# Layer 1's head periods: an SSM tile's turn counts and lag products move ahead in the vector queue, and the second tile's expansion drops its wait for the first

## What is computed

```
for l in range(DEPTH):                       # two layers
    h = rms_norm(x, norm_g[l]); z = h @ w_in[l]
    ... o_na, o_dl, o_m: 6 + 6 + 4 heads ...
    x = x + concat(o * silu(gate)) @ w_out[l]
# second block, s5_mixer:
ab = exp(lam * dt)                           # 64 groups x 64 states, complex
bu = B_bar u;  s_t = ab * s_(t-1) + bu_t;  y = C s + d_skip * u
```

## Time and profile before

| what | value |
|---|---|
| median of 3 runs | 2592.64 us (2587.49 to 2593.14) |
| the profiled execution's own time | 2586.36 us |
| its span | 2584.7 us |
| PE busy | 2476.3 us, 96% of the span |
| DVE, ACT, POOL busy | 65%, 47%, 24% |
| chain that ended last | PE 69%, DVE 15%, issue 7%, ACT 5% |
| head periods of layer 1 | about 552 to 1030 us |
| PE busy there (552 to 1024) | 441.55 of 472 us, granted clock 0.97 |

### The profile page before, as it was taken

One profiled execution on the slowest core, in us unless ns is written; L12 is line 12 of the kernel. 1 busy time (PEld: TensorE's weight loads), 2 busy tenths in 40 slices (PEclk: granted clock), 3 DMA queues, 4 the chain that ended last, 5 costly groups with the idle time before them and its releaser, 6 DMA issues.

```text
span 2584.7 us, 50520 instructions
## 1 busy us (share of the span) xinstructions
PE 2476.3 (96%) x18072; PEld 2348.0 (91%) x18072; DVE 1691.9 (65%) x2556; ACT 1220.9 (47%) x1819; POOL 628.6 (24%) x1047
## 2 busy tenths in 40 slices
PE   7999999989999999999988999999999999999999
PEld 7899999989899999998888999999888888888888
DVE  7876666567777777667777766565555555555555
ACT  5344544445555555555665434444544444444443
POOL 3300031358778886220010222011000000000000
PEclk9999999999999999999999999999999999999999
DMA  6655575555555555555454777565666676767764
GB/s 234 209 181 195 175 221 178 186 173 174 166 177 182 186 184 188 159 165 191 141 169 152 234 234 239 201 218 173 191 191 187 187 187 186 186 186 187 187 185 157
DMA packets 217449, 484.85 MB, mean 188 GB/s; under 512 B 22760, under 2 KB 120724, under 8 KB 217088
## 3 DMA queue, kind: packets, MB, share of 16 engines
q1 hardware_dynamic: 182912, 415.29, 52.6%
q0 software_dynamic: 13216, 37.93, 4.7%
q10 hardware_dynamic: 21216, 30.22, 3.6%
HBM read 455.00 MB, written 31.08 MB: 188 GB/s over the span
## 4 chain that ended last, share of the span: by engine, by line
PE 69%; DVE 15%; issue 7%; ACT 5%; POOL 2%; ACTq 1%; DVEq 0%; DMA 0%; POOLq 0%
PE z_ps L1987 12%; PE z_ps L1988 12%; PE z_ps L1989 12%; PE z_ps L2323 6%; PE z_ps L2324 6%; PE z_ps L2329 6%; DVE w_lo L1297 5%; ACT w_hi L717 2%; PE o_ps L2358 1%; PE o_ps L2357 1%; PE o_ps L2356 1%; PE v_ps L2357 1%; PE v_ps L2356 1%; PE p_ps L2357 1%; PE v_ps L2358 1%
## 5 line engine op out<-in xcount | busy, mean ns | idle before, releaser
L1297 DVE TENSOR_TENSOR w_lo<-w_raw,w_hi 128x1024 fp32r<-128x1024 f32 x520 | 634.8, 1249 | 335.4 <-ACT w_hi L717 333.1
L1987 PE MATMUL z_ps<-x_hi,w_hi 128*128 128x256 f32 x2816 | 822.1, 292 | 16.9 <-DVE w_lo L1290 14.4
L1988 PE MATMUL z_ps<-x_lo,w_hi 128*128 128x256 f32 x2816 | 805.3, 286 | 0.0
L1989 PE MATMUL z_ps<-x_hi,w_lo 128*128 128x256 f32 x2816 | 804.9, 286 | 0.0
L717 ACT ACTIVATE w_hi<-w_raw 128x1024 fp32r<-128x1024 f32 x520 | 533.1, 1051 | 262.5 <-PE z_ps L1989 216.5
L1987 PEld LDWEIGHTS z_ps<-x_hi,w_hi 128*128 128x128 f32 x2816 | 549.0, 195 | 26.9 <-issue 18.8
L1988 PEld LDWEIGHTS z_ps<-x_lo,w_hi 128*128 128x128 f32 x2816 | 549.3, 195 | 1.0
L1989 PEld LDWEIGHTS z_ps<-x_hi,w_lo 128*128 128x128 f32 x2816 | 548.9, 195 | 0.0
L1877 DVE TENSOR_TENSOR w_lo<-w_raw,w_hi 128x1024 fp32r<-128x1024 f32 x262 | 320.8, 1225 | 314.8 <-ACT w_hi L1141 314.7
L1141 ACT ACTIVATE w_hi<-w_raw 128x1024 fp32r<-128x1024 f32 x262 | 277.7, 1060 | 427.9 <-PE z_ps L2329 272.5
L2323 PE MATMUL z_ps<-w_hi,x_hi 128*128 128x512 f32 x704 | 275.1, 391 | 0.6 <-DVE res L1853 0.6
(11 more groups left out here) (382 smaller groups left out, 4131.5 us busy)
## 6 DMA issues: line engine op xcount, KB each, us to landing
w_raw<-in_w SPq DMA_DIRECT2D x704, 512.0 KB, 4.3
w_raw<-in_w SPq DMA_DIRECT2D x80, 384.0 KB, 4.8
res<-tab_d POOLq DMA_DIRECT2D x32, 384.0 KB, 4.5
w_raw<-in_w SPq DMA_DIRECT2D x80, 128.0 KB, 2.9
tab_d<-arena ACTq DMA_DIRECT2D x32, 256.0 KB, 2.1
tab_d<-arena POOLq DMA_DIRECT2D x32, 128.0 KB, 3.4
sg_d<-arena ACTq DMA_DIRECT2D x32, 128.0 KB, 4.6
arena<-sg_d POOLq DMA_DIRECT2D x16, 256.0 KB, 3.8
```

Of the source, the lines that this page charges most:

```text
L1297: dve.tensor_tensor(w_lo[:, n % RING, :], w_raw[:, n % RING, :], w_hi[:, n % RING, :].bitcast(F32), ALU.subtract).then_inc(w_lo_ready, 1)
L1987: pe.matmul(z, wh, hi[:, kt, :], start=(first and i == 0), stop=False)
L1988: pe.matmul(z, wh, lo[:, kt, :], start=False, stop=False)
L1989: m = pe.matmul(z, wl, hi[:, kt, :], start=False, stop=(last and i == len(kts) - 1))
```

## The change

VectorE's `tile` is split into `tile_turns` (the five turn instructions with their wait for `tab_ready`) and `tile_lags` (the waits for `e_ready`, `bt_ready`, `tab_stored` and the four lag products). In layer 1, `tile_turns(2h)` now stands before `split_lo(p, 2)`; `tile_lags(2h, 0)` right behind `split_lo(p, 3)`, so before `softmax_scale` and the evacuation of job 1; `tile_turns(2h+1)` takes the place of the old even tile, before `split_lo(p, 4)`; `tile_lags(2h+1, 1)` stays at the end. In period 0 the even tile's lag products stand right behind `split_lo(p, 2)`, and ScalarE's even tile is moved up behind `split_hi(p, 2)`. PE's tile waits for the copies and lag products of the tile before the last (`st - 1`) and no longer of the last one. No instruction that computes is added or dropped.

```diff
@@ scalar, head_period
                 split_hi(p, 2)
+                if norm and l == 1:
+                    tile(0, 0)
                 if prev:
                     softmax_exp(g - 1, prev and not prev2)
                 split_hi(p, 3)
...
-                if l == 1:
+                if l == 1 and not norm:
                     tile(2 * h, 0, last)
                 split_hi(p, 4)
@@ vector
-            def tile(st, e, last=False):
-
-                k_ps = tile_bank(z_ps[3 - 2 * e])[1]
+            def tile_turns(st):
+
                 reach(dve, tab_ready, st)
...
                 dve.tensor_scalar(turns, turns, 0.5, -0.5, ALU.min, ALU.max).then_inc(turns_ready, 1)
+
+            def tile_lags(st, e, last=False):
+
+                k_ps = tile_bank(z_ps[3 - 2 * e])[1]
                 dve.wait_ge(e_ready, st + 1)
@@ vector, head_period
                     evac(gate_z[:], p - 1, 3, rstd[:])
+                if l == 1:
+                    tile_turns(2 * h)
                 split_lo(p, 2)
+                if norm and l == 1:
+                    tile_lags(0, 0)
...
                     split_lo(p, 3)
+                    if l == 1:
+                        tile_lags(2 * h, 0, last)
                 if prev:
                     softmax_scale(g - 1)
...
                 if l == 1:
-                    tile(2 * h, 0, last)
+                    tile_turns(2 * h + 1)
                 split_lo(p, 4)
                 evac(q_t[:] if kind == "mem" else v_t[:], p, 2, rstd[:])
...
                 if l == 1:
-                    tile(2 * h + 1, 1, last)
+                    tile_lags(2 * h + 1, 1, last)
@@ tensor, tile
                 pe.wait_ge(xt_step, 15 * st + 15)
-                reach(pe, e_ready, st)
-                reach(pe, m_ready, st)
+                reach(pe, e_ready, st - 1)
+                reach(pe, m_ready, st - 1)
```

## The result

The changed kernel takes **2556.58 us** (median of 4 runs, 2554.59 to 2557.47) against 2591.56 us before (4 runs, 2587.49 to 2593.14): ratio 0.9866, 95% interval 0.9849 to 0.9883. The forecast was 2560.5 us. The profiled execution took 2556.99 us with a span of 2555.3 us, for 2586.36 and 2584.7 before.

A forecast was written before the change was run, and what follows sets the result against it. PE was taken to bound the kernel, waiting at the odd tile for VectorE's lag products of the even one. Savings of 22.4 - 0.5 + 8.3 + 1.9 = 32.1 us gave 2592.6 - 32.1 = 2560.5 us, range 2552 to 2574.

The forecast's parts named there:

- the sum: Whole execution: 22.4 - 0.5 + 8.3 + 1.9 = 32.1 us saved, all passing to the end.
- The releaser: PE's odd tile in layer 1: VectorE's `m_ready` of the even tile ends the wait, though the profile mostly names POOL.
- The 15 waits: PE's odd-tile waits in the head periods after period 0: 22.4 us to go, 0.5 us kept for remains.
- the margin of 0.3 us at the bank: Job 1's bank in period 2: seen free at 633.5, PE there at 633.79, so no wait.
- Rival (a): Rotary periods: waits re-form, about 2.4 us plus two clock falls of 1.6 us each; 2566 us, chance 0.13.
- the signs: Changed kernel's profile: every head period from 1 on 27.8 to 28.1 us long at a clock of 1.00.
- The clock: PE in periods 1, 2, 3, 5, 8: no fall to 1.2 GHz once waits go, 8.3 us back.
- rival (b): PE's clock in the head periods doesn't recover, the link to waits being loose; 8.3 us missing, 2569 us, chance 0.09.
- Period 0: First head period: PE's odd tile starts at 571.95 for 573.81, saving 1.9 us; the wait of 6 us stays.
- the remains: Odd-tile waits in the head periods after period 0: 0.5 us expected to stay, bounds 0 and 2.4 us.
- rival (c): Late in layer 1 POOL becomes the bound at 15.0 us a tile; PE waits 9.6 us, about 2570, chance 0.06.
- The slower rival (e): VectorE's lag products wait for ScalarE's copy of B, L735; 3.5 us late means 39 us of PE waits, 2607, chance 0.06.

The follow-up runs named there:

- Experiment 2: Kernel before with only PE's two waits at the tile relaxed to `st - 1`, VectorE's order unchanged: 2587.16 us, ratio 0.9977.
- experiment 3: Kernel before with only VectorE's turns moved as in the change, lag products still behind the evacuation, PE's waits as before: 2559.07 us, ratio 0.9874.
- experiment 1: Changed kernel with PE's old waits at the tile put back (`st` for `st - 1`), new order kept: 2555.71 us, ratio 0.9867.
- Experiment 7: Changed kernel with PE's odd tile, from period 1 on, also waiting for VectorE's lower half of the next chunk: 2603.2 us.
- experiment 9: Changed kernel with ScalarE's even tile taking its sines ahead of its copies, so the copy of B comes later: 2579.72 us, ratio 0.9951.
- experiment 4: Kernel before with turns moved as in the change, lag products behind the evacuation, PE's waits relaxed to `st - 1`: 2563.76 us, ratio 0.9889.
- experiment 5: Kernel of experiment 4 with GpSimd's last multiplication of each tile replaced by a memset, leaving out the highest power: 2552.3 us.
- experiment 8: Changed kernel; in period 0 PE's odd tile stands behind job 3 and VectorE splits the next chunk before that tile's turns: 2559.10 us, ratio 0.9869.

## Why the prediction was right

The forecast stood 4 us above the median measured, and the wait that it named was the one that counted. The medians differ by 35.0 us (2591.56 and 2556.58) where 32.1 were forecast; the head stretch and the tail, 32.5 + 3.0 us, account for that. That the head stretch alone came so near to 32.1 is in part luck, since errors of over 1 us each way cancelled in it (below, at the sum). Point by point:

- **The releaser.** "`m_ready` of the even tile, and not POOL": right. Experiment 2 takes it off the tile (with the wait for the copies, which end at 629.4 in period 2, long before) and the odd tile's waits go (2.0 us in 3 are left outside period 0), with POOL untouched; experiment 3 leaves it in place, makes it earlier, and they go too, to 0.8 us or less. But the reason that the order is the change and PE's waits are not (experiment 1) was not seen: the sum put the gain on the wait taken off PE's list.
- **The 15 waits.** 22.4 us forecast to go, 0.5 to remain; 1.75 us remain in four rotary periods (0.52, 0.43, 0.39, 0.41), and in the ten without only the 0.23 of period 6, for the load of B, which the other two profiles of the changed kernel don't have. The step that was mis-sized is the margin of 0.3 us at the bank, worked out from period 2: in period 4 the bank is free 0.4 us too late. Ahead of it stand 1.24 us of lag products, counted at 1.22, and beside them some 0.5 us of small things that were taken as fixed: the pair of lower halves 2.40 us from its start to the next instruction's for 2.28, their start 0.18 later, and 0.80 for 0.56 from L1370 to the evacuation. Rival (a), then, is what happened in small: 1.75 us, and no fall of the clock behind waits of 0.4. Nor are the periods 27.8 to 28.1 us long, as the signs had it: 28.2 to 28.3 in periods 2 to 5, 27.6 from period 7 on.
- **The clock.** 8.3 us forecast back: periods 1 to 15 are at 1.00. Experiment 7 shows the link by putting waits in again; in experiment 9 the clock reads 0.94 or 0.95 in four of the five rotary periods, where the waits sum to 1.4 to 1.8 us, and 1.00 where they are 0.8. The link is loose, as rival (b) said: the fifth rotary period there, with the same 1.8, reads 1.00, as did ten of the 15 periods with a wait in the kernel before.
- **Period 0.** 571.95 forecast, 571.78 measured, by the steps named: the norm slipped 1.23 us for the 1.1 worked out, and the wait of 6.04 us stayed.
- **The sum** of 32.1 us: at the last tile the lead is 32.6 (1022.38 for 989.78), with the remains 1.25 larger than forecast, period 0 better by 0.2, and some 1.5 us the other way that the working had not: it took period 6's 27.76 us of PE busy for the floor, and eight periods are 27.6.
- **What was left out**: the tail, 3 us, and the stage of `inputs` and `outputs`, which took 9.8 back in the profiled execution. Two stretches without a line of the change, ahead of that stage and behind it, were 0.8 and 2.8 us shorter in this execution, and all of it together brought the difference of the profiled times to 29.4.
- **GpSimd**, rival (c), was given 0.06 and taken at 0. Its stores had 7.1 us in hand at tile 4, 2.9 at tile 18 and 1.2 at tile 31, so 0 was right by a small distance. The premise was not: a tile on POOL has no length of its own. It takes 13.8 us late in the changed kernel (14.4 to 14.7 between tiles 12 and 18 of the same run) and 14.8 in experiment 4, by where VectorE's `w_lo` fall, and one place in VectorE's queue decides. The row of 2.39 us in the earlier trace rows, read as one instruction, is two (x2) of 1.20 and 1.23 us; in the changed kernel, at 577.97 and away from `w_lo`, the same two take 0.26 and 0.25, so what the row was to show stands all the same. The Trainium skill (SBUF — State Buffer, section "SBUF: two separate sides") has the two engines hold a shared pair of ports in turn; the shapes of experiment 4 agree.
- **The slower rival (e)**: not what happened, as ScalarE's L735 ends at 652.57 in period 3 of the changed kernel (the expectation of experiment 9 calls it period 2) and VectorE comes at 653.50. Experiment 9 prices it: 1.8 to 2.0 us of waiting on VectorE cost 26.2 us of stretch. The rival's estimate (24 us lost from 2.5 us of lateness on) came near by two errors: the periods without rotary pass on less than it said, and the clock, which it left out, makes up for it.

No kernel here beats the change by more than its interval. The best that computes everything is the changed kernel itself, which experiment 1 equals; a shorter period 0 or the order of experiment 4 would need a GpSimd that is some 1 us a tile faster first (an estimate, from the 14.8 and 13.8 us of a tile), and with one multiplication less (experiment 5) the order of experiment 4 shows 434.5.

## What to carry to other kernels

When one wait holds two engines together, move the work that releases it in its own queue before relaxing the wait: the order alone gave the whole gain, the relaxed wait alone 0.2%. Look up who waits for the same semaphore next, because a wait that is taken off one instruction reappears there. And before filling a gap, ask which engine off the path runs at full load: its durations may depend on the phase to another engine, so a step moved by 2 us can make it the bound.

## What the runs showed of the hardware

- The same GpSimd instruction (128x64, f32) takes 0.58 or 1.25 us on the mean, by whether its place falls beside VectorE's `w_lo` (single ones 0.45 and 2.08, experiment 4); a pair of tiles takes 27.6 or 29.5.
- Waits of 1.7 us at the odd tile brought a fall of PE's clock in most periods (0.94 and 1.5 us more busy, experiment 7), those of 1.5 to 2.5 in the kernel before in four of eight. At the even tile seven waits of 1.7 us (experiment 4) and three of 1.4 to 1.7 (experiment 8) brought none, but one of 1.51 us did (experiment 3: 0.94, 29.10 us busy). So it isn't the place alone, and what decides is open.
- A wait costs more than its length, even at a clock that reads 1.00: in periods of experiment 9 with a wait of 0.76 us PE is busy 28.0 us, in those of the changed kernel with a wait of 0.4 to 0.5 it is 27.8, and in those without one 27.6 (from one even tile to the next).
- The profile names POOL for odd tiles of the kernel before that VectorE released (experiment 2 takes most of these waits away with POOL's work as it was), and names it rightly in experiment 4. The instruction that ends 0.05 to 0.35 us before the waiting one starts is the better witness (0.26 and 0.24 in the earlier trace rows, 0.34 at the even tile of experiment 4).
